# The chunked scan of a two-model forward pass: raw scores crossed and state kept by GpSimd, and the second product of the triangular inverse as one 128-row matmul per head pair

## The reference

```python
def rwkv7_scan(r, w, k, v, a_vec, b_vec):
    def step(S, inp):
        r_t, w_t, k_t, v_t, a_t, b_t = inp
        sa = jnp.einsum('bhvk,bhk->bhv', S, a_t)
        S = S * w_t[:, :, None, :] + sa[..., None] * b_t[:, :, None, :] + v_t[..., None] * k_t[:, :, None, :]
        y = jnp.einsum('bhvk,bhk->bhv', S, r_t)
        ...
```

## Time and profile before

| | |
|---|---|
| median of 3 runs | 3722.22 us |
| the profiled execution's own time | 3716.17 us |
| its span, first to last instruction | 3714.4 us |
| TensorE busy over the span | 3506.0 us (94%) |
| VectorE, ScalarE, GpSimd busy | 2565.7, 1568.9, 1186.1 us |
| mean granted TensorE clock | 0.973 of 2.4 GHz |
| the scan | from about 1602 to 1928 us, 19 periods |

### The profile page before, as it was taken

How to read it: one execution, slowest core, us unless ns; L and a number is a source line. 1 busy time by engine, 2 the same in 40 slices (tenths; PEclk the granted TensorE clock), 3 DMA queues, 4 the chain that set the end, 5 groups by cost and what they waited for, 6 DMA issues and landing times. The chain is left out here.

```text
span 3714.4 us, 51957 instructions
## 1 busy us (share of the span) xinstructions
PE 3506.0 (94%) x21892; PEld 2858.9 (77%) x21892; DVE 2565.7 (69%) x2294; ACT 1568.9 (42%) x1868; POOL 1186.1 (32%) x544
## 2 busy tenths in 40 slices
PE   8999999999999998979888999999998999997996
PEld 6778788887877776668876788887877888886875
DVE  5563776678766875868766666678767888857532
ACT  5563533334443336857665433334444222125322
POOL 1125445445532211244433454545531000000221
PEclk9999999999999999979999999999999999998998
DMA  2112123354313233853423123354312222234322
GB/s 102 46 46 65 60 91 112 101 184 136 116 51 104 74 134 110 250 167 88 115 61 118 60 91 111 102 185 138 115 53 95 80 85 69 80 125 107 144 91 108
DMA packets 227447, 387.30 MB, mean 104 GB/s; under 512 B 33216, under 2 KB 127552, under 8 KB 223232
## 3 DMA queue, kind: packets, MB, share of 16 engines
q1 hardware_dynamic: 189648, 311.62, 26.5%
q10 hardware_dynamic: 37568, 72.36, 5.3%
HBM read 277.50 MB, written 105.91 MB: 103 GB/s over the span
## 5 line engine op out<-in xcount | busy, mean ns | idle before, releaser
L3940 POOL MEMSET ssm_toep<- 128x4096 f32 x1 | 3.5, 3513 | 539.0 <-POOLq L3606 539.0
L3467 DVE SCALAR_TENSOR_TENSOR H<-hy_cu,par,H 128x1024 f32<-128x1024 f32 x120 | 153.4, 1279 | 0.0
L270 POOL TENSOR_TENSOR wlo1C<-fast_raw,whi1C 128x1024 fp32r<-128x1024 f32 (+1 forms) x40 | 111.1, 2777 | 112.8 <-ACT whi1C L260 112.8
L270 POOL TENSOR_TENSOR wlo0B<-fast_raw,whi0B 128x1024 fp32r<-128x1024 f32 (+1 forms) x40 | 112.0, 2801 | 107.6 <-ACT whi0B L260 107.6
L270 POOL TENSOR_TENSOR wlo1A<-fast_raw,whi1A 128x1024 fp32r<-128x1024 f32 (+1 forms) x40 | 111.5, 2787 | 105.3 <-ACT whi1A L260 105.3
L270 POOL TENSOR_TENSOR wlo1B<-fast_raw,whi1B 128x1024 fp32r<-128x1024 f32 (+1 forms) x39 | 108.9, 2792 | 113.2 <-ACT whi1B L260 113.2
L270 POOL TENSOR_TENSOR wlo0A<-fast_raw,whi0A 128x1024 fp32r<-128x1024 f32 (+1 forms) x40 | 110.1, 2752 | 104.8 <-ACT whi0A L260 104.8
L3467 DVE SCALAR_TENSOR_TENSOR hy_odd<-hy_cu,par,hy_odd 128x1024 f32<-128x1024 f32 x112 | 143.2, 1279 | 0.0
L1008 DVE TENSOR_TENSOR fast_xl<-fast_xr,fast_xh 128x2048 fp32r<-128x2048 f32 (+1 forms) x42 | 127.7, 3062 | 20.9 <-ACT fast_xh L849 20.9
L270 POOL TENSOR_TENSOR wlo0C<-fast_raw,whi0C 128x1024 fp32r<-128x1024 f32 (+1 forms) x39 | 108.0, 2769 | 104.4 <-ACT whi0C L260 104.4
L2965 DVE STREAM_TRANSPOSE sc_XT<-sc_XX 64x512 f32<-64x512 f32 x160 | 112.9, 706 | 35.2 <-POOL sc_XX L2922 30.5
(11 more groups left out here) (1458 smaller groups left out, 11550.5 us busy)
## 6 DMA issues: line engine op xcount, KB each, us to landing
fast_raw<-ffn_in_dram SPq DMA_DIRECT2D x88, 512.0 KB, 3.8
fast_xr<-ffn_x SPq DMA_DIRECT2D x28, 1024.0 KB, 5.8
fast_raw<-ffn_out_dram SPq DMA_DIRECT2D x32, 512.0 KB, 3.7
sc_ops<-rw_arbkv SPq DMA_DIRECT2D x14, 1024.0 KB, 6.1
wraw1A<-hybrid_in_dram SPq DMA_DIRECT2D x24, 512.0 KB, 3.4
wraw1B<-hybrid_in_dram SPq DMA_DIRECT2D x24, 512.0 KB, 3.5
ffn_x<-fast_g ACTq DMA_DIRECT2D x22, 512.0 KB, 3.2
ffn_x<-fast_e ACTq DMA_DIRECT2D x22, 512.0 KB, 2.8
```

Of the source, the lines that this page charges most:

```text
L270: eng.tensor_tensor(self.slot(wlo, n), self.raw[n], self.slot(whi, n).bitcast(fp32), ALU.subtract)\
L3467: op = dve.scalar_tensor_tensor(out=acc, in0=c[:, j:j + T], scalar=w, in1=acc, op0=ALU.mult, op1=ALU.add)
L3940: pl.memset(toep[:, :, :], 0.0).then_inc(*tick("st_zero"))
```

## The change

1. `Wt[l]` gets a column block per head, `[P, DT, 2, CHUNK]`: `w_out` writes head e's rows into head e's columns, and the rest stays at the zeros that GpSimd wrote at the start. `spread` becomes one matmul per tile with a stationary of 128 rows by 128 columns and 32 moving columns on 128 rows: 8 matmuls instead of 16.
2. ScalarE's `to_xx` is gone. GpSimd's `begin` reads `G` crosswise itself, in two instructions of 64 partitions, multiplied with the first mask on the way; the identity is added after that as before.
3. The update of `S` goes from VectorE (3003) to GpSimd (`keep`, after slot 1's level), `S` has one buffer, and `out_of_state` reads the decayed state out of `UV` instead of `S`.
4. In even periods ScalarE does both pairs of B's `time_out` before `w_out(step(n, 4))`.
5. `Z` has one buffer, `NT` four instead of five, tiles are placed anew, and the zeroing of levels 1 to 4 moves behind the first `begin`. The load of A into `G` waits also for GpSimd's crossing.

```diff
-                self.Z = at("sc_Z", [P, 2, DT, HEAD], fp32, 64)
+                self.Z = at("sc_Z", [P, DT, HEAD], fp32, 64)
...
-                self.NT = at("sc_NT", [P, 5, DT, CHUNK], fp32, 133.25)
-                self.Wt = [at(f"sc_Wt{l}", [P, DT, CHUNK], fp32, k) for l, k in enumerate((144.25, 146.25, 150.25, 68, 70))]
+                self.NT = at("sc_NT", [P, 4, DT, CHUNK], fp32, 133.25)
+                self.Wt = [at(f"sc_Wt{l}", [P, DT, 2, CHUNK], fp32, k) for l, k in enumerate((144.25, 172.25, 148.25, 176.25, 68))]
...
-            NTS = 5
+            NTS = 4
...
                     def load_a(n):
-                        sp.wait_ge(*after("sc_raw", 4 * n + 4))
+                        sp.wait_ge(*after("sc_raw", 2 * n + 2))
+                        sp.wait_ge(*after("sc_first", 2 * n + 2))
...
                         for m in range(DT):
-                            for e in range(2):
-                                mx = pe.matmul(part_of_tile(eight[2 + ix % 2][half(e), m, :], lx, 1), Wt[lx][half(e), m, :],
-                                               part_of_tile(XX[half(e), cx % 4, m, :], lx, 1), start=True, stop=True)
+                            mx = pe.matmul(part_of_tile(eight[2 + ix % 2][:, m, :], lx, 1), Wt[lx][:, m, :, :],
+                                           part_of_tile(XX[:, cx % 4, m, :], lx, 1), start=True, stop=True)
...
-                        pe.wait_ge(*after("sc_S", n + 1))
+                        pe.wait_ge(*after("sc_SU", 2 * n + 2))
...
-                                mm = pe.matmul(eight[place(("y", n))][half(e), m, :], S[half(1 - e), a, m, :],
+                                mm = pe.matmul(eight[place(("y", n))][half(e), m, :], UV[half(1 - e), n % 4, e, m, :],
...
-                                act.activation(part_of_two(Wt[l][half(e), q:DT:2, :], l), part_of_two(paired[i % 2][half(q), e, :, :], l),
+                                act.activation(part_of_two(Wt[l][half(e), q:DT:2, e, :], l), part_of_two(paired[i % 2][half(q), e, :, :], l),
...
-                    def to_xx(n):
...
-                            act.activation(XX[half(e), n % 4, :, :], G[half(1 - e), n % 4, e, :, 0:CHUNK], ACT.Copy).then_inc(*tick("sc_raw"))
...
-                        if chunk(n + 1):
-                            to_xx(n + 1)
...
-                        w_out(step(n, 4))
                         if turned_in(n, 2):
                             for a in range(2):
                                 time_out(*turned_in(n, 2), 1, a)
+                        w_out(step(n, 4))
...
                     def begin(n):
                         x = XX[:, n % 4, :, :]
-                        pl.wait_ge(*after("sc_raw", 4 * n + 2))
-                        pl.tensor_tensor(x, x, by_m(sfirst[:, :]), ALU.mult).then_inc(*tick("sc_first"))
-                        pl.wait_ge(*after("sc_first", n + 1))
+                        pl.wait_ge(*gone(("score", n, 1, 1)))
+                        if n >= 4:
+                            pl.wait_ge(*after("pe_U", n - 3))
...
+                        for e in range(2):
+                            if e == 1:
+                                pl.wait_ge(*after("sc_first", 2 * n + 1))
+                            pl.tensor_tensor(XX[half(e), n % 4, :, :], G[half(1 - e), n % 4, e, :, 0:CHUNK], by_m(sfirst[:, :])[half(1 - e), :, :],
+                                             ALU.mult).then_inc(*tick("sc_first"))
+                        pl.wait_ge(*after("sc_first", 2 * n + 2))
                         pl.tensor_tensor(x, x, by_m(seye[:, :]), ALU.add).then_inc(*tick("sc_eye_added"))
...
+                    def keep(n):
+                        pl.wait_ge(*gone(("S", n)))
+                        pl.tensor_tensor(S[:, :, :], grown[:, :, :], pc[:, :, n:n + 1].to_broadcast([P, DT, HEAD]), ALU.mult)\
+                          .then_inc(*tick("sc_S"))
...
+                            if j == 1 and chunk(n - 3) and n - 3 < NC - 1:
+                                keep(n - 3)
...
-                        dve.tensor_tensor(S[:, 1 - a, :, :], grown[:, :, :], pc[:, :, n:n + 1].to_broadcast([P, DT, HEAD]), ALU.mult)\
-                           .then_inc(*tick("sc_S"))
```

More of the change, by code:

```diff
@@ L2546, in rwkv_scan @@
             STEPS = ((0, 0), (1, 2), (2, 4), (0, 1), (1, 3))
+            LAG = {l: back for back, l in STEPS}
             def half(e):
@@ L2760, in u_step @@
                             for e in range(2):
-                                mm = pe.matmul(eight[place(("U", n))][half(1 - e), m, :], XX[half(e), n % 4, m, :], Z[half(e), n % 2, m, :],
+                                mm = pe.matmul(eight[place(("U", n))][half(1 - e), m, :], XX[half(e), n % 4, m, :], Z[half(e), m, :],
                                                start=True, stop=True)
@@ L2831, in w_out, with to_gx @@
                             for e in range(2):
[L2832 removed]
+                                act.activation(part_of_two(Wt[l][half(e), q:DT:2, e, :], l), part_of_two(paired[i % 2][half(q), e, :, :], l),
                                                ACT.Copy).then_inc(*tick("sc_W"))
[L2835 removed]
+                    def to_gx(n):
                         act.wait_ge(*gone(("score", n, 1, 1)))
[L2837 to L2842 removed]
                         if n == 2:
@@ L2861, in z_out @@
                             act.wait_ge(*after("op_out_ab_0", 0))
-                        act.activation(Z[:, n % 2, :, :], eight[place(("Z", n))], ACT.Copy).then_inc(*out(("Z", n)))
+                        if n >= 1:
+                            act.wait_ge(*after("pe_U", n))
+                        act.activation(Z[:, :, :], eight[place(("Z", n))], ACT.Copy).then_inc(*out(("Z", n)))
                     def u_out(n):
@@ L2913, in zero @@
                     def zero(l):
-                        pl.wait_ge(*after(("op_out_ks_0", "op_out_ks_0", "op_out_ks_1", "op_out_ab_1", "op_out_ab_1")[l], 0))
-                        pl.memset(Wt[l][:, :, :], 0.0).then_inc(*tick("sc_zero"))
+                        pl.wait_ge(*after(("op_out_ks_0", "op_out_aa_1", "op_out_ks_1", "op_out_aa_1", "op_out_ab_1")[l], 0))
+                        if l >= 1:
+                            pl.wait_ge(*after("scan_in_b", 144))
+                        pl.memset(Wt[l][:, :, :, :], 0.0).then_inc(*tick("sc_zero"))
                     def begin(n):
                         x = XX[:, n % 4, :, :]
-                        pl.wait_ge(*after("sc_raw", 4 * n + 2))
-                        pl.tensor_tensor(x, x, by_m(sfirst[:, :]), ALU.mult).then_inc(*tick("sc_first"))
-                        pl.wait_ge(*after("sc_first", n + 1))
+                        pl.wait_ge(*gone(("score", n, 1, 1)))
+                        if n >= 4:
+                            pl.wait_ge(*after("pe_U", n - 3))
+                        if n == 0:
+                            pl.wait_ge(*after("sc_zero", 1))
+                        else:
+                            pl.wait_ge(*after("sc_NT", max(i for (c, l), i in order.items() if c + LAG[l] < n) + 1))
+                        for e in range(2):
[4 more added lines that the diff above has]
+                        pl.wait_ge(*after("sc_first", 2 * n + 2))
                         pl.tensor_tensor(x, x, by_m(seye[:, :]), ALU.add).then_inc(*tick("sc_eye_added"))
@@ L2942, in _ @@
                             if n == 0 and j == 0:
-                                for l in range(2, LEVELS):
+                                for l in range(1, LEVELS):
                                     zero(l)
+                            if j == 1 and chunk(n - 3) and n - 3 < NC - 1:
+                                keep(n - 3)
                         if chunk(n + 1):
@@ L2995, in state_out @@
                         dve.wait_ge(*after("sc_S", n + 1))
-                        dve.tensor_tensor(grown[:, :, :], eight[place(("S", n))], S[:, a, :, :], ALU.add).then_inc(*out(("S", n)))
+                        dve.tensor_tensor(grown[:, :, :], eight[place(("S", n))], S[:, :, :], ALU.add).then_inc(*out(("S", n)))
                         dve.wait_ge(*gone(("S", n)))
@@ L3015, in _ @@
                         x_out(before(n, 0))
+                        if n == 2:
+                            dve.wait_ge(*after("op_out_ab_0", 0))
+                            dve.memset(S[:, :, :], 0.0).then_inc(*tick("sc_S"))
                         if chunk(n - 3) and n - 3 < NC - 1:
@@ L3035, in rwkv_scan @@
             passed({"sc_W": 4 * len(order), "sc_clear": 1})
-            passed({n: NC for n in ("sc_first", "sc_eye_added", "pe_Z", "pe_U", "pe_ys", "pe_y", "sc_S")})
+            passed({n: NC for n in ("sc_eye_added", "pe_Z", "pe_U", "pe_ys", "pe_y", "sc_S")})
             passed({"pe_S": NC - 1})
```

11 lines of the change are left out of this document (4 added, 7 removed).

## The result

The changed kernel takes 3780.61 us (median of 4 runs, 3780.32 to 3781.37) against 3719.99 us for the kernel before (4 runs, 3712.75 to 3722.61): ratio 1.0173, 95% interval 1.016 to 1.0187 (the medians alone divide to 1.0163, inside that interval). It is slower, as forecast, by 60.6 us, where 38 were forecast. The profiled execution took 3780.32 us with a span of 3778.2 us, 63.8 us over the span before.

What follows compares the result with a forecast made beforehand. TensorE was taken as the bound wherever it doesn't wait. Twelve periods at 20.9 instead of 18.8 us (+25), start +8 and tail +5 gave +38 us, forecast 3760 us; own range 3735 to 3788, 8-in-10 range 3696 to 3790.

Steps and rivals of the forecast that it cites:

- The spread's price: TensorE's spread: 16 records with 128-column loads at 112 ns each, 1.79 us, +0.86 us per spread.
- B: Rival: the 128-column load is as quick as the transposes' own, spread 1.02 us, total 3704 us; chance 0.13.
- C: Rival: TensorE records cost the same whatever their form, so half the records take half the time, 3681 us; chance 0.13.
- M: Rival in between: pace near 80 ns, +0.35 us per spread, the change's two halves cancel, 3721 us; chance 0.08.
- The long wait on ScalarE: Even periods: V's transposes wait 2.5 us for ScalarE's copies of B's second half; claimed to go, with the clock's fall.
- The steady period: Scan's twelve steady periods: 20.9 us each instead of 18.8, from 16.1 us of TensorE work plus spreads, +25 us.
- changes of form: TensorE: score, out_of_state and u_step behind a spread each pay 0.12 us for a new matmul form, 0.36 us per period.
- The start: Before the twelve periods: about 11 spreads at 1.3 us more, 14 us, of which 8 were taken.
- The tail: Behind the twelve periods: 9 spreads at 0.86 us more, 8 us, of which 5 were taken.
- A TensorE that waits for GpSimd's `NT`: Named sign of a wrong forecast: TensorE waiting for GpSimd's `NT`; no size given.
- Nothing for it: GpSimd's `keep` as a new wait ahead of slots 2 to 4: costed at nothing, `NT` fitting by 0.2 us.
- GpSimd's prices: GpSimd's `begin` and `keep`: 1.27 us taken for each instruction, 2.15 us kept for the crossing; 11.5 us work per period.

Runs made afterwards that it cites:

- 64-column form: The changed kernel with each spread as two matmuls per tile, 128 rows by 64 columns, instead of one: 3712.35 us, ratio 0.999.
- ScalarE's order alone: The kernel before, with one edit: in even periods ScalarE does both pairs of B's copies before slot 4's `w_out`: 3704.27 us, ratio 0.9967.
- Both experiments that take `keep` out of the levels' way: The changed kernel with the update of S behind its period's levels, 3771.5 us, and with that update back on VectorE, 3760.24 us.
- `keep` late: GpSimd's update of S moved behind its period's levels: 3771.5 us on the changed kernel, 3703.96 us with the spread also as two 64-row matmuls.
- two-half kernels: The changed kernel with spreads as two 64-row matmuls: 3721.62 us; also with S's update behind the levels, 3703.96 us, or on VectorE, 3705.32 us.
- first two-half kernel: The changed kernel with the spread taken back to two 64-row matmuls per tile, all else as changed: 3721.62 us, ratio 1.0015.
- light loads: Scan operand loads after the first pair cut to an eighth, with two 64-row spread matmuls and S's update behind the levels: 3697.43 us, ratio 0.9946.

## Why the prediction was right or wrong

**The spread's price** was taken right: 112 ns per record forecast, 113 measured, so 1.81 us of TensorE's time for 16 records where 1.79 were forecast. The columns of the stationary operand set it, as the step of 52 to 57 ns in the earlier trace rows said: with the same 32 moving columns, 64-column loads go at 29 ns. The Trainium skill (TensorE: Matmul & The Clock Gate, LDWEIGHTS) counts only columns and gives 107 ns for 128 of them; the trace agrees at 2.4 GHz, with 113, and the 1.08 us of the 64-column form shows that rows don't count. At 1.2 GHz the trace has 213 ns, twice the page's figure. With that, cases B, C and M fell: L2706's own load, the row against, was the wrong neighbour, and the fixed price per record doesn't hold for this form.

**The long wait on ScalarE** is gone, and so is the fall of the clock behind it (1.00 in both periods): right. ScalarE's order alone shows its worth, 11 us.

**The steady period** was forecast at 20.9 us and is 20.5. Twelve periods gave +20.3 instead of +25. Two errors of opposite sign lie in it. The spreads and the changes of form were priced too low: u_step with its spread, from the spread's start to the transposes, takes 1.81 us before and 2.99 after.

```profile
1753.02 0.95 PE L2733 MATMUL psB<-sc_XX,sc_Wt 64*64 64x32 f32 x26
...
1754.83 0.27 PE L2706 MATMUL psD<-sc_eye,sc_ops 64*128 64x64 f32 x1
```

```profile
1692.55 1.97 PE L2734 MATMUL psB<-sc_XX,sc_Wt 128*128 128x32 f32 x16
1694.46 1.15 PE L2762 MATMUL psC<-sc_Z,sc_XX 64*64 64x64 f32 x32
1695.54 0.27 PE L2708 MATMUL psD<-sc_eye,sc_ops 64*128 64x64 f32 x1
```

That is +1.18. Out_of_state gives +1.17, score +0.99, and zed +0.85, read the same way at the full clock and without a wait; the spread ahead of state, where a wait stood before, is taken like zed's. Together that is +5.0 per period where 5 x 0.86 + 0.36 = 4.7 were forecast. Beyond the 0.88 of the spread itself (16 x 113 ns less 32 x 29) score pays 0.1 for its change of form, as forecast, but u_step and out_of_state pay 0.3 each. So the 16.1 us of work was too high: 20.5 less 5.0 leaves about 15.5. The 16.1 came from one odd period less 1.0 us of waits, and its granted clock of 0.98 says that some of it still ran at the lower level.

**The start** was +12.7 instead of +8. Six of its eleven spreads take 3.62 us, against 1.92 at that clock in the earlier trace rows, one takes 2.27, four 1.97. Of 11 x 1.3 = 14 us I had let TensorE's waits hide six; 12.7 measured leave little that they can have hidden. No run separated it. That the 4.7 us too few here and the 4.7 too many in the twelve periods cancel is luck.

**The tail** is the step that failed: +5 forecast, +26.6 measured, and 4.2 more behind the start of the next stage, which the sum didn't have at all. A TensorE that waits for GpSimd's `NT` was named as a sign of being wrong, and here it stands, though GpSimd isn't the bound: it waits itself, 14.89 us for `grown`. "Nothing for it" was said of `keep` from one steady pair, where the `NT` of slot 2 is in time by 0.2 us. For the steady periods of the changed kernel that held: no wait for `NT` stands there. In the last periods the scores and transposes of further chunks are gone, and nothing covers the way from `grown` over `keep` to the levels behind it. `keep` ties the inverse's levels to the state's chain, two chains that had been side by side. The clock falls behind the three waits, and at 1.2 GHz a spread costs 3.62 us. Both experiments that take `keep` out of the levels' way start the next stage 15.7 us earlier, and the second gives back 20 us in all, nearly the whole difference between the measured +60.6 and the forecast +38. Without `keep` the tail is still 10.8 us over the kernel before, where 5 were forecast for its long spreads. Why 4.2 us are lost behind the tail is open: the one execution traced with `keep` late starts the next stage at the same low clock and loses 1.7.

**The relief of case B** was over-counted as well, which the forecast itself didn't feel, since the long spread covered everything. With short spreads the change is worth +6 us, not -18: the margin of 0.2 us is used up (3.4 us of waits for `NT` ahead of 1884 us, 10.2 behind it, in the tail), and a TensorE without its long wait meets "issue" idle time instead, 14.3 us. With `keep` out of the way 11 us of gain are left, ScalarE's.

**Of GpSimd's prices** the crossing was right (64 partitions, 1.27 us):

```profile
L2925 POOL TENSOR_TENSOR sc_XX<-sc_G,sc_first 64x512 f32<-64x512 f32 x28 | 35.5, 1267 | 30.9 <-DVE sc_G L2971 29.8
L2943 POOL TENSOR_TENSOR sc_S<-sc_grown,rw_pc 128x512 f32<-128x512 f32 x13 | 20.3, 1562 | 94.7 <-DVE sc_grown L3008 94.7
```

`keep` was not: 1.56 us instead of 1.27 (the mean stands behind the busy time), and the level behind it up to 1.71. The last section shows what ran beside it.

## What to carry to other kernels

Two small products merged into one block-diagonal matmul halve the records but double the columns of the stationary operand; where few columns stream past it, price the load (here 29 ns per record side by side against 113); filling up the rows with zeros cost nothing, filling up the columns took the spread from 1.1 to 1.97 us. A new wait in front of an engine's list must be priced also in the first and last periods, where the work that hid it is gone, and with the clock that can fall behind such a wait. Before a step is moved to another engine, try the order on the engine it is on: here one line moved on ScalarE gave 11 us, and no combination of the other parts on top of it was better by more than the intervals allow. A sum that comes out near can hide errors that cancel: compare it with the trace stretch by stretch.

## What was not expected of the hardware

**VectorE and GpSimd side by side.** `UV` and `keep` read the same two tiles at the same moment, and both stretch. VectorE's two `UV` instructions take 2.15 us beside `keep` (0.69 for the first, 1.43 for the second) and 1.40 us where the update is on VectorE (the two-half kernels, `keep` late and update on VectorE):

```profile
1681.02 2.15 DVE L3016 TENSOR_TENSOR sc_UV<-sc_grown,rw_pc 64x512 f32<-64x512 f32 x2
```

```profile
1695.27 1.40 DVE L3012 TENSOR_TENSOR sc_UV<-sc_grown,rw_pc 64x512 f32<-64x512 f32 x2
```

The Trainium skill (GPSIMD Engine Reference, Specifications) says that GpSimd shares its SBUF interfaces with VectorE and contends with instructions that have two SBUF inputs; the trace agrees, with 0.75 us on VectorE and 0.3 us on GpSimd, though the first of the two `UV` instructions, under `keep` for all of its time, doesn't stretch. The same tiles aren't needed for it: in the kernel before the update of `S` on VectorE took 1.76 us instead of 0.68 the one time that it ran beside a level of GpSimd, at 1895.65. `grown`, which reads one operand from PSUM, stays at 0.69 us; in the changed kernel GpSimd stands still meanwhile, but in the kernel before five of 15 run nearly wholly beside a busy GpSimd. In the steady periods of the changed kernel the stretch was hidden, in the tail it was not.

**TensorE stops with everything ready.** In the first two-half kernel it stood for 2.78 us in the middle of u_step, between two records of one group that wait for nothing. The windows around that gap and the DMA queues of 1684 to 1693 us (packets, MB, share):

```profile
1688.00:1690.20 2.20, 2.20 (x73) 1.96 (x69) 0.81 (x2) 2.10 (x5) 2.15 (x2) 1.00 1.07 364
1690.20:1693.00 2.80, 0.04 (x1) 0.00 (x0) 2.43 (x4) 2.15 (x6) 1.57 (x2) 0.80 0.21 67
...
q1 hardware_dynamic: 2043, 2.06, 71.6%
q8 instruction: 1, 0.02, 0.7%
```

The gap follows a stretch in which a load fills the DMA engines (1.07, 364 GB/s), and among 2043 packets of data there is one of instructions. An eighth of the bytes took most of these gaps away and 6.5 us of time; the changed kernel, with 408 to 424 records in a period where this two-half kernel has 486 to 504, has no such gap in its steady part.

The packets' own times in the traces tie the gaps to the instructions. Queue 8 brings them in packets of 16 KB, in the two-half kernels every 4.4 us in the median. The one of this gap begins 7.15 us after the one before it and lands at 1691.68; TensorE goes on at 1693.02, 1.34 us later. It is the same with all 83 "issue" gaps of 0.3 us or more that end between 1660 and 1915 us, in the kernel before and the eight experiments with short spreads: each ends 1.2 to 1.8 us after such a packet has landed, and the packet came 4.2 to 8.3 us after the one before. Between 1661 and 1850 us, with full loads (two halves, `keep` late), 8 of the distances between packets are over 5.5 us, the longest 6.5; with light loads 2 are, the longest 5.8. In the changed kernel most are over 5.5 us, up to 8.4, and TensorE doesn't stop: at 20 records per us it uses up its list more slowly than the two-half kernels, which reach 28.

So that TensorE stands for want of instructions there is borne out by the order of events in nine traces. That it is the load's packets which hold the instructions up is argued: the light loads, the only run that bears on it, took the gaps away, but gave about half or less of the time that was expected of them.
